# Router of a top-2 expert layer: root and reciprocal, merged comparisons, column ranks by four matmuls, the first expert's table from its rank and its rows normed ahead of the gates

## The reference

```python
def layer_norm(x, g, b):
    mu = jnp.mean(xf, axis=-1, keepdims=True)
    var = jnp.mean(jnp.square(xf - mu), axis=-1, keepdims=True)
    return (xf - mu) * lax.rsqrt(var + LN_EPS) * g + b

def moe_swiglu(x, w_router, w_gu, w_down):
    logits = (x @ w_router).astype(jnp.float32)
    top_v, top_i = lax.top_k(logits, TOP_K)
    gates = jax.nn.softmax(top_v, axis=-1)
    combine = jnp.einsum('...k,...ke->...e', gates, jax.nn.one_hot(top_i, N_EXPERTS, dtype=jnp.float32))
    y = jnp.zeros_like(x)
    for e in range(N_EXPERTS):
        y = y + swiglu(x, w_gu[e], w_down[e]) * combine[..., e:e + 1].astype(x.dtype)
    return y
```

## Time and profile before

| | us |
|---|---|
| median of three runs | 1629.1 |
| lowest and highest | 1629.02, 1629.2 |
| the profiled execution | 1628.6 |
| its span | 1626.9 |
| TensorE busy | 1565.4 (96%) |
| VectorE busy | 1289.1 (79%) |
| ScalarE busy | 1052.6 (65%) |
| GpSimd busy | 100.0 (6%) |

### The profile page before, as it was taken

How to read it: one execution, slowest core, us unless ns; L and a number is a source line. 1 busy time by engine, 2 the same in 40 slices (tenths; PEclk the granted TensorE clock), 3 DMA queues, 4 the chain that set the end, 5 groups by cost and what they waited for, 6 DMA issues and landing times.

```text
span 1626.9 us, 23673 instructions
## 1 busy us (share of the span) xinstructions
PE 1565.4 (96%) x8972; PEld 1359.5 (84%) x8972; DVE 1289.1 (79%) x1301; ACT 1052.6 (65%) x964; POOL 100.0 (6%) x154
## 2 busy tenths in 40 slices
PE   8899998999999999999999999999999999999995
PEld 7789987999999997887887887887887887887883
DVE  5786544678546768889889889889889889889896
ACT  5984333766325455777777777777777777777772
POOL 3105000011000011000000000000000000003000
PEclk9999998999999999999999999999999999999998
DMA  9747603689555546999999999999999999999990
GB/s 277 224 131 258 246 2 122 192 269 304 193 180 182 177 136 254 383 372 353 384 371 354 382 370 353 383 368 356 381 370 354 382 370 355 383 370 352 392 397 38
DMA packets 227446, 476.66 MB, mean 293 GB/s; under 512 B 9692, under 2 KB 69100, under 8 KB 227081
## 3 DMA queue, kind: packets, MB, share of 16 engines
q1 hardware_dynamic: 216040, 435.66, 74.7%
q0 software_dynamic: 11344, 40.12, 7.5%
HBM read 449.74 MB, written 26.24 MB: 293 GB/s over the span
## 4 chain that ended last, share of the span: by engine, by line
PE 88%; ACT 6%; DVE 4%; issue 1%; DMA 0%; DVEq 0%; SPq 0%; ACTq 0%
PE bank L2026 13%; PE bank L2025 13%; PE bank L2029 13%; PE bank L2054 12%; PE bank L383 6%; PE bank L2060 6%; PE bank L394 6%; PE bank L384 6%; ACT high L345 2%; DVE low L350 1%; PE bank L1756 1%; PE bank L1777 1%; PE bank L2037 1%; PE bank L1909 1%; PE bank L1910 1%; PE bank L1915 1%
## 5 line engine op out<-in xcount | busy, mean ns | idle before, releaser
L350 DVE TENSOR_TENSOR low<-raw,high 128x2048 fp32r<-128x2048 f32 x405 | 923.4, 2290 | 177.3 <-ACT high L345 176.9
L345 ACT ACTIVATE high<-raw 128x2048 fp32r<-128x2048 f32 x405 | 774.6, 1917 | 322.7 <-PE bank L2029 98.3
L2025 PE MATMUL bank<-high,xgh 128*128 128x512 f32 x896 | 358.8, 400 | 0.7 <-DVE xgl L1528 0.7
L2026 PE MATMUL bank<-high,xgl 128*128 128x512 f32 x896 | 355.2, 396 | 0.0
L2029 PE MATMUL bank<-low,xgh 128*128 128x512 f32 x896 | 245.7, 396 | 0.0
L383 PE MATMUL bank<-xhb,high 128*128 128x266 f32 (+1 forms) x832 | 221.8, 298 | 10.2 <-ACT xhb L821 7.6
L384 PE MATMUL bank<-xlb,high 128*128 128x266 f32 (+1 forms) x832 | 215.4, 290 | 0.0
L2029 PEld LDWEIGHTS bank<-low,xgh 128*128 128x128 f32 x896 | 168.8, 188 | 41.3 <-DVE low L350 0.3
L2025 PEld LDWEIGHTS bank<-high,xgh 128*128 128x128 f32 x896 | 168.7, 188 | 39.1 <-issue 0.9
L2026 PEld LDWEIGHTS bank<-high,xgl 128*128 128x128 f32 x896 | 168.7, 188 | 38.7
L383 PEld LDWEIGHTS bank<-xhb,high 128*128 128x128 f32 x832 | 161.3, 194 | 12.5 <-issue 9.9
(11 more groups left out here) (399 smaller groups left out, 1535.8 us busy)
## 6 DMA issues: line engine op xcount, KB each, us to landing
raw<-in_moe_w_gu_dram SPq DMA_DIRECT2D x224, 1024.0 KB, 5.4
raw<-in_moe_w_down_dram SPq DMA_DIRECT2D x112, 1024.0 KB, 5.7
raw<-in_ffn_w_gu_dram SPq DMA_DIRECT2D x22, 1024.0 KB, 6.0
raw<-in_gdn_w_in_dram SPq DMA_DIRECT2D x16, 1024.0 KB, 11.0
tok<-zeros POOLq DMA_DIRECT2D x26, 512.0 KB, 18.1
raw<-in_sc_w_in_dram SPq DMA_DIRECT2D x12, 1024.0 KB, 5.1
raw<-in_ffn_w_down_dram SPq DMA_DIRECT2D x11, 1024.0 KB, 5.0
s<-in_state_gdn_S_dram POOLq DMA_DIRECT2D x8, 512.0 KB, 7.2
```

The source lines that it names most:

```text
L345: eng.activation(high[:, n % SPLIT, :], raw[:, n % RAW, :], ACT.Copy).then_inc(high_ready, 1)
L350: eng.tensor_tensor(low[:, n % RAW, :], raw[:, n % RAW, :], high[:, n % SPLIT, :].bitcast(F32), ALU.subtract).then_inc(low_ready, 1)
L2025: pe.matmul(out, xgh[:, 4 * kh + k, :], wh[:, k, :], start=kh + k == 0, stop=False)
L2026: pe.matmul(out, xgl[:, 4 * kh + k, :], wh[:, k, :], start=False, stop=False)
```

## The change

The reciprocal root becomes ScalarE's Sqrt and VectorE's reciprocal; the six xn operations go by column half first. The comparisons of the three token groups become two operations whose results stand side by side, so that one reduction adds both; the selection is one operation. `sel` gets a fourth group of zeros, and four products count the columns, into bank 5 instead of 3; TensorE waits for three xn operations before. `last0` is the place of a token in the first expert's table straight from the ranks, and the table is written ahead of the other rank work. The first half of the gathered rows is normed and split ahead of the gates, the second half behind them, and the low split of `MOE0 + 2` with the two waits behind it moves there too. TensorE fills with `keep_dense` (products of 512 columns) four and three times instead of 24 and 12 transposes, has no filling behind the gathering, waits for the halves of xn one by one, and waits for the halves of the first rows at the slots that need them (it does so for every expert).

```diff
@@ -199,12 +199,12 @@
 tab_at = region + 60 * D
 JOBS = EX * TILES
 logits = place("logits", [128, 3, EX], at=tab_at)
-sel = place("sel", [128, 3, EX], at=tab_at + 96)
+sel = place("sel", [128, 4, EX], at=tab_at + 5920)
+last0 = place("last0", [128, 3], at=tab_at + 96)
 gates = place("gates", [128, 3, EX], at=tab_at + 192)
 rank = place("rank", [128, 3, EX], at=tab_at + 288)
 valid = place("valid", [128, 3, EX], at=tab_at + 384)
-cmp_gt = place("cmp_gt", [128, 3, EX, EX], at=tab_at + 480)
-cmp_eq = place("cmp_eq", [128, 3, EX, EX], at=tab_at + 1248)
+cmp = place("cmp", [128, 3, EX, 2, EX], at=tab_at + 480)
 before = place("before", [128, EX, EX], at=tab_at + 2016)
 top = place("top", [128, 3], at=tab_at + 2272)
 total = place("total", [128, EX], at=tab_at + 2304)
@@ -624,6 +624,7 @@
                             base=-1, pattern=[[1, EX], [-1, EX]], channel_multiplier=0))
     step(pool.tensor_copy(seat[:, :], seat_i[:, :]))
     step(pool.memset(flag[:, :], 0.0))
+    step(pool.memset(sel[:, 3, :], 0.0))
     step.wait()
     pool.tensor_copy(ebase[:, :], ebase_i[:, :]).then_inc(const_ready, 1)
     pool.wait_ge(slot_used, MOE0)
@@ -936,15 +937,13 @@
         split_high(act, n + SPLIT)
         for k in range(2 * (n - SCO0) + 2, min(2 * (n - SCO0) + 4, KT)):
             norm_shift(1, k)
-    act.preload_act_table_set("natural_log")
+    act.preload_act_table_set("sqrt_and_others")
     act.wait_ge(var_ready, 1)
-    act.activation(rstd_n[:, :], moments[:, :, 1], ACT.Ln, bias=eps[:, 1:2]).then_inc(log_ready, 1)
-    act.wait_ge(log_ready, 1)
-    act.activation(rstd_n[:, :], rstd_n[:, :], ACT.Exp, scale=-0.5).then_inc(rstd_ready, 1)
+    act.activation(rstd_n[:, :], moments[:, :, 1], ACT.Sqrt, bias=eps[:, 1:2]).then_inc(rstd_ready, 1)
     act.wait_ge(nmr_ready, 1)
     act.wait_ge(const_ready, 8)
-    for tt in range(3):
-        for h in range(2):
+    for h in range(2):
+        for tt in range(3):
             p = 128 if tt < 2 else NS
             act.activation(xn[0:p, tt, 512 * h:512 * h + 512], bank[row_bank(tt, h)][0:p, :], ACT.Identity,
                            scale=rstd_n[0:p, tt:tt + 1], bias=nmr[0:p, tt:tt + 1]).then_inc(xn_ready, 1)
@@ -1423,6 +1422,8 @@
     ins.then_inc(var_ready, 1)
     dve.wait_ge(var_ready, 1)
     dve.wait_ge(rstd_ready, 1)
+    step(dve.reciprocal(rstd_n[:, :], rstd_n[:, :]))
+    step.wait()
     dve.scalar_tensor_tensor(nmr[:, :], moments[:, :, 0], -1.0, rstd_n[:, :], ALU.mult, ALU.mult).then_inc(nmr_ready, 1)
     dve.wait_ge(nmr_ready, 1)
     for tt in range(3):
@@ -1435,45 +1436,41 @@
                                       over[0:p, 0, tt, :], ALU.mult, ALU.add))
     step.wait()
     step(dve.tensor_reduce(top[:, :], logits[:, :, :], X, ALU.max))
-    for tt in range(3):
-        mine = logits[:, tt, :].rearrange("p (e o) -> p e o", o=1).to_broadcast([128, EX, EX])
-        other = logits[:, tt, :].rearrange("p (o e) -> p o e", o=1).to_broadcast([128, EX, EX])
-        step(dve.tensor_tensor(cmp_gt[:, tt, :, :], other, mine, ALU.is_gt))
-        step(dve.tensor_tensor(cmp_eq[:, tt, :, :], other, mine, ALU.is_equal))
+    mine = logits[:, :, :].rearrange("p t (e o) -> p t e o", o=1).to_broadcast([128, 3, EX, EX])
+    other = logits[:, :, :].rearrange("p t (o e) -> p t o e", o=1).to_broadcast([128, 3, EX, EX])
+    step(dve.tensor_tensor(cmp[:, :, :, 1, :], other, mine, ALU.is_equal))
+    step(dve.tensor_tensor(cmp[:, :, :, 0, :], other, mine, ALU.is_gt))
     step.wait()
     dve.tensor_tensor(gates[:, :, :], logits[:, :, :], top[:, :].rearrange("p (t o) -> p t o", o=1)
                       .to_broadcast([128, 3, EX]), ALU.subtract).then_inc(top_ready, 1)
+    step(dve.tensor_tensor(cmp[:, :, :, 1, :], cmp[:, :, :, 1, :], before[:, :, :].rearrange("p (o e) f -> p o e f", o=1)
+                           .to_broadcast([128, 3, EX, EX]), ALU.mult))
+    step.wait()
+    step(dve.tensor_reduce(rank[:, :, :], cmp[:, :, :, :, :].rearrange("p t e a f -> p t e (a f)"), X, ALU.add))
+    step.wait()
+    dve.scalar_tensor_tensor(sel[:, 0:3, :], rank[:, :, :], 1.5, valid[:, :, :], ALU.is_lt, ALU.mult).then_inc(sel_ready, 1)
+    dve.wait_ge(sel_ready, 1)
+    dve.wait_ge(rank_psum, 1)
+    step(dve.scalar_tensor_tensor(last0[:, :], bank[5][:, 0:24].rearrange("p (t e) -> p t e", t=3)[:, :, 0], float(CAP),
+                                  sel[:, 0:3, 0], ALU.add, ALU.mult))
+    step.wait()
     for tt in range(3):
-        step(dve.tensor_tensor(cmp_eq[:, tt, :, :], cmp_eq[:, tt, :, :], before[:, :, :], ALU.mult))
-    step.wait()
-    step(dve.tensor_tensor(cmp_gt[:, :, :, :], cmp_gt[:, :, :, :], cmp_eq[:, :, :, :], ALU.add))
-    step.wait()
-    step(dve.tensor_reduce(rank[:, :, :], cmp_gt[:, :, :, :], X, ALU.add))
-    step.wait()
-    step(dve.tensor_scalar(sel[:, :, :], rank[:, :, :], 1.5, None, ALU.is_lt))
-    step.wait()
-    dve.tensor_tensor(sel[:, :, :], sel[:, :, :], valid[:, :, :], ALU.mult).then_inc(sel_ready, 1)
-    split_low(dve, MOE0 + SPLIT - 1)
-    dve.wait_ge(xn_ready, 6)
-    dve.wait_ge(vec_in, 64)
-    dve.wait_ge(rank_psum, 1)
-    step(dve.tensor_tensor(rank[:, :, :], bank[3][:, 0:24].rearrange("p (t e) -> p t e", t=3),
+        ins = dve.tensor_scalar(onehot[:, tt, :], seat[:, :], last0[:, tt:tt + 1], None, ALU.is_equal)
+    ins.then_inc(onehot_ready, 1)
+    step(dve.tensor_tensor(rank[:, :, :], bank[5][:, 0:24].rearrange("p (t e) -> p t e", t=3),
                            ebase[:, :].rearrange("p (o e) -> p o e", o=1).to_broadcast([128, 3, EX]), ALU.add))
     for k in range(1, TILES):
-        step(dve.tensor_scalar(over[:, k - 1, :, :], bank[3][:, 0:24].rearrange("p (t e) -> p t e", t=3),
+        step(dve.tensor_scalar(over[:, k - 1, :, :], bank[5][:, 0:24].rearrange("p (t e) -> p t e", t=3),
                                CAP * k + 0.5, CAP * (EX - 1.0), ALU.is_gt, ALU.mult))
-    step(dve.tensor_reduce(most[:, 0:1], bank[3][:, 24:32], X, ALU.max))
+    step(dve.tensor_reduce(most[:, 0:1], bank[5][:, 24:32], X, ALU.max))
     step.wait()
     for k in range(1, TILES):
         step(dve.tensor_tensor(rank[:, :, :], rank[:, :, :], over[:, k - 1, :, :], ALU.add))
         step.wait()
-    step(dve.tensor_tensor(last_at[:, :, :], rank[:, :, :], sel[:, :, :], ALU.mult))
-    step(dve.tensor_scalar(first_at[:, :, :], sel[:, :, :], -65536.0, 65536.0, ALU.mult, ALU.add))
-    step.wait()
-    for tt in range(3):
-        ins = dve.tensor_scalar(onehot[:, tt, :], seat[:, :], last_at[:, tt, 0:1], None, ALU.is_equal)
-    ins.then_inc(onehot_ready, 1)
+    step(dve.tensor_tensor(last_at[:, :, :], rank[:, :, :], sel[:, 0:3, :], ALU.mult))
+    step(dve.tensor_scalar(first_at[:, :, :], sel[:, 0:3, :], -65536.0, 65536.0, ALU.mult, ALU.add))
+    step.wait()
     step(dve.tensor_tensor(first_at[:, :, :], first_at[:, :, :], last_at[:, :, :], ALU.add))
     step(dve.tensor_reduce(row_f[:, 1, :], last_at[:, :, :], X, ALU.max))
     step.wait()
@@ -1490,8 +1487,28 @@
     step.wait()
     dve.tensor_scalar(rounds_i[0:1, 1:2], most[0:1, 3:4], float(EX), -1.0, ALU.mult, ALU.add).then_inc(tiles_ready, 1)
+    def normed(jobs, g):
+        dve.wait_ge(xg_psum, jobs * 2 + (g + 1))
+        for d in range(4 * g, 4 * g + 4):
+            ins = dve.tensor_scalar(xf[:, d, :], heads(2 + g)[:, d % 4, :], vecs[:, d, 2:3], vecs[:, d, 6:7],
+                                    ALU.mult, ALU.add)
+        ins.then_inc(xf_ready, 1)
+    def low_half(jobs, g):
+        dve.wait_ge(xgh_ready, jobs * 2 + (g + 1))
+        dve.tensor_tensor(xgl[:, 4 * g:4 * g + 4, :], xf[:, 4 * g:4 * g + 4, :], xgh[:, 4 * g:4 * g + 4, :].bitcast(F32),
+                          ALU.subtract).then_inc(xgl_ready, 1)
+    def gathered(jobs):
+        for g in range(2):
+            normed(jobs, g)
+        for g in range(2):
+            low_half(jobs, g)
+    normed(0, 0)
+    low_half(0, 0)
     dve.wait_ge(ex_ready, 1)
-    step(dve.tensor_tensor(gates[:, :, :], gates[:, :, :], sel[:, :, :], ALU.mult))
+    step(dve.tensor_tensor(gates[:, :, :], gates[:, :, :], sel[:, 0:3, :], ALU.mult))
     step.wait()
     step(dve.tensor_reduce(top[:, :], gates[:, :, :], X, ALU.add))
     step.wait()
@@ -1515,20 +1532,11 @@
     step.wait()
     step(dve.scalar_tensor_tensor(gate_bm[:, :], seat_b[:, :], 0.5, gate_ab[:, 1, :], ALU.is_lt, ALU.mult))
     step(dve.tensor_scalar(seat_b[:, :], seat_b[:, :], float(CAP), None, ALU.add))
-    def gathered(jobs):
-        for g in range(2):
-            dve.wait_ge(xg_psum, jobs * 2 + (g + 1))
-            for d in range(4 * g, 4 * g + 4):
-                ins = dve.tensor_scalar(xf[:, d, :], heads(2 + g)[:, d % 4, :], vecs[:, d, 2:3], vecs[:, d, 6:7],
-                                        ALU.mult, ALU.add)
-            ins.then_inc(xf_ready, 1)
-        for g in range(2):
-            dve.wait_ge(xgh_ready, jobs * 2 + (g + 1))
-            dve.tensor_tensor(xgl[:, 4 * g:4 * g + 4, :], xf[:, 4 * g:4 * g + 4, :], xgh[:, 4 * g:4 * g + 4, :].bitcast(F32),
```

(36 more changed lines are left out.)

## The result

The changed kernel takes 1632.62 us (median of 11 executions, 1629.89 to 1635.73) against 1629.02 of the kernel before on the same chip (11, 1625.08 to 1630.75): ratio 1.0029, interval 1.0020 to 1.0037. The ratio takes in all executions and lies near that of the means (1633.21 against 1628.36), while the medians alone give 1.0022. The range of the prediction ended at 1630.8.

The account below looks back on a forecast made before the run. It took TensorE as the bound, held in the router by VectorE's serial chain. 5.5 us gained less 3.7 of new wait and 1.5 of low clock left 0.3, so 1628.8 us, range 1625.8 to 1630.8.

Parts of the forecast that it names:

- Root and reciprocal: Router, ahead of the logits: second table load goes, logits start 0.44 us earlier; the gates' own table load is hidden.
- Merged comparisons: VectorE from logits to selection: fewer operations save 0.79 us, leaving 2.55.
- Ranks: TensorE behind the selection: four products instead of nine take 1.3 us instead of 2.37, bounds 1.05 and 1.8.
- acc in front of the fourth slot's low part: VectorE, first expert: low part behind acc ready only at 632.93, so TensorE waits and gives back 3.7 us.
- The clock behind the pause: First expert, behind TensorE's 3.7 us wait: granted clock of 0.5 for 3.4 us, costing 1.5 us.
- the step on the clock ahead of the ranks: Router, between logits products and ranks: clock may still be 0.5 when the selection arrives; only a rival, chance 0.25.
- its own second version: Slower rival with low clock through ranks (+0.9) and first half of the gathering (+1.4): 1631.1 us.
- The 1.4 for half a gathering: Cost in us assumed for the gathering's first half, 4.2 us long, if the clock stays at 0.5.
- the pause: TensorE's wait for the fourth slot's low part in the first expert: 3.7 us, with a low clock behind it.
- The slower rival: Clock at 0.5 from before the ranks, delaying VectorE's chain: 1629.7 or 1631.1 us, chance 0.25.

Follow-up runs that it names:

- e3: Changed kernel with 6 instead of 4 dense products ahead of the selection; ratio to the kernel before 1.0005.
- e5: Changed kernel with 12 and 8 transposes as filling and the third slot's low split back behind the selection; ratio to the kernel before 0.9983.
- e1: Changed kernel with all TensorE filling as before (24, 12 and 20 transposes); ratio to the kernel before 1.0006.
- e4: Kernel before with only its filling changed to 4 and 3 dense products, none behind the gathering; ratio to the kernel before 1.0065.
- e14: Changed kernel with 16 transposes between the two halves of the gathering; ratio to the kernel before 1.0043.
- e6: Changed kernel with 12 and 8 transposes, low split back behind the selection, acc moved into the first expert's slots; ratio to the kernel before 0.9971.
- e10: Changed kernel with 12 and 8 transposes and acc in the first expert's slots, low split as changed; ratio to the kernel before 0.9960.
- e9: Changed kernel with 12 and 14 transposes, low split back behind the selection, acc in the first expert's slots; ratio to the kernel before 0.9974.
- e12: Changed kernel with 6 and 5 dense products and acc in the first expert's slots, low split as changed; ratio to the kernel before 0.9979.
- e13: Changed kernel with 20 and 14 transposes and acc in the first expert's slots, low split as changed; ratio to the kernel before 0.9966.
- e8: Changed kernel with its own 4 and 3 dense products, low split back behind the selection, acc in the first expert's slots; ratio to the kernel before 1.0014.
- e11: Changed kernel with 9 instead of 3 dense products behind the ranks; ratio to the kernel before 1.0028.

## Why the prediction was wrong, point by point

**Right.** What bounds the router and what each step of the chain costs while the clock is high. Root and reciprocal: the logits wait 0.73 us for their products, so little was to be had; they start 4.16 us behind the start of the products instead of 4.84, 0.68 gained where I had 0.44; the table load is hidden. Merged comparisons: 2.51 against 2.55. Ranks: 1.3 predicted, 2.11 at half clock, 1.69 in e3 with the clock rising within them; in e5, at full clock, the four products end 1.17 us behind the selection. acc in front of the fourth slot's low part: with the clock repaired e3 has that low start 26.05 us after the logits (631.32 less 605.27), 25.73 was the sum, and TensorE's pause is 3.40, 3.7 was predicted. The clock behind the pause fell as said, but its price did not hold: 1.5 us in the sum, taken from a stretch of 3.4 us, and 2.7 in e3, whose stretch at 0.50 lasted 6.8. The forecast (1628.8 against 1629.1, a ratio of 0.9998) was in effect that of e1 and e3 (1.0006 and 1.0005), a little too low for that reason.

**Wrong: the step on the clock ahead of the ranks.** "After, 4 large matmuls stand there and then TensorE is idle until 607.5" was seen, and priced as a rival with a chance of 0.25; in the sum of the forecast it stands at nothing. Two things failed. The chance: I counted against it that four matmuls keep TensorE busy to 606.6 and three more follow. They did so (605.45 is 6.13 us behind the start of the logits products, 606.6 was 6.08), the idle time before the ranks is 0.69, and the clock does not come back; e3 shows that with two more it can (in its profile), e4 that this filling alone costs 0.65% in the kernel before. The size: the rival gave the low clock 0.9 us for the ranks and 1.4 for the first half of the gathering, because the stretch of 0.50 that I took as measure lasted 3.4 us and the gathering is unbroken work. (The trace before has a longer one, 245.5 to 255.7 us; a pause of 7.6 us ends in it at 250.9, and the 4.8 us of work behind that are at 0.50 too. I left it out.) In the changed kernel the low clock lasted 27 us. Both halves of the gathering went at 0.57 of their speed (+6.4 us, where I had +1.4), and the first slot and the start of the second with it. Nor did the range fit this rival: it ended at 1630.8, below the 1631.1 of its own second version, and gave what lies beyond 0.04. The 1.4 for half a gathering was itself too small: the factor 7/4, which I wrote beside it, gives 3.1, and 7.40 in e14 against 4.2 is that.

**Less than feared: the pause.** Because TensorE came later, the wait for the low part was 0.92 us (1.4 for the weight load) instead of 3.7, and no low clock followed. The rule of the Trainium skill (TensorE: Matmul & The Clock Gate, "HAM oscillation — how this bites in real kernels") that waits between bursts put the array back to half rate is borne out by the pauses of e3 and e14 (3.40 us each); the changed kernel's loss had another form, a clock that did not come back under unbroken work.

**Sum, as it should have stood**, counted from the logits products. To the first expert: 2.65 gained up to the gathering, 6.41 lost in it, 3.10 gained behind it (the 2.40 of transposes and the 0.70 of waiting for xgl), together 0.66 lost. From there to the fourth slot's low part 14.27 us instead of 10.40: 2.4 lost in the first slot and 0.4 in the second at half clock, 1.1 by the wait for the low part. Together 4.5. The slower rival, whose mechanism this is in part, gave 1631.1; 1632.6 came.

## What to carry to other kernels

When filling is shortened because the chain beside it got shorter, ask whether the clock is back before the next costly products begin, and read the granted clock there in more than one execution: in the profiles of e1, e3 and e6 it was back once TensorE had no gap between the logits products and the ranks, in that of e10 it was not. A gain on TensorE's side is worth no more than the slack of the engine that feeds it next and what that engine gains itself: here VectorE had 1.5 us of slack and, in e3, had the low part 0.5 us earlier (631.24 less 600.52 against 631.32 less 601.11 for its start, counted from the logits products); together they are the 1.95 that e3 gained up to there. 7 us of work that nobody needed until the end (acc) stood in front of what TensorE waited for. More filling together with another order on VectorE (e6, e9, e10, e12, e13) turns 0.3% slower into 0.2 to 0.4% faster than the kernel before; more filling alone (e1 to e3) and the other order alone (e8) do not.

## What the runs showed of the hardware that I had not expected

Work that holds the clock does not always raise it. In the kernel before the gathering (48 instructions of 128 columns, 8.48 us) runs at 1.00 from end to end; once the clock is at 0.50 as it begins (in e5, 0.3 us behind its start), the same instructions without a gap leave it there for 14.8 to 15.0 us (changed kernel, e4, e5, e8, e10, e11), while behind 16 transposes of the unit matrix it is back (e14), and in those six profiles it is back 3 to 9 us behind the gathering's end, in the first slots of the expert. Which property of the gathering does this, its table of zeros and ones or its float32 form, was not tried. So a fall at the wrong moment costs 6.4 us in the gathering and 10 us in the whole (e5: 1622 to 1626 or 1633 to 1636 us for one program). And the clock can fall without any pause: in every profile of this case it falls in or just behind the logits products (columns of 8, 4 us without a gap).
